# Eight experts in two stripes of 1792 columns: longer weight runs, eight slots of 14 KB, equal column groups

## What is computed

```python
def swiglu(h, w1, w3, w2):
    return (jax.nn.silu(h @ w1) * (h @ w3)) @ w2

def moe_ffn(h, router_w, w1, w3, w2):
    logits = (h @ router_w).astype(jnp.float32)
    vals, idx = lax.top_k(logits, TOP_K_EXPERTS)
    probs = jax.nn.softmax(vals, axis=-1)
    gate = jnp.sum(jax.nn.one_hot(idx, N_EXPERTS, dtype=jnp.float32) * probs[..., None], axis=-2)
    out = jnp.zeros_like(h)
    for e in range(N_EXPERTS):
        out = out + gate[..., e:e + 1] * swiglu(h, w1[e], w3[e], w2[e])
    return out
```

## Time and profile before

| | |
|---|---|
| Time, median of 3 runs | 1609.66 us (1607.83 to 1609.97) |
| Profiled execution, its own time | 1608.24 us |
| Its span, first to last instruction | 1606.5 us |
| Granted TensorE clock, mean | 0.992 |
| PE busy | 1569.4 us (98%) |
| DVE / ACT / POOL busy | 854.8 / 390.4 / 407.1 us |
| Moved by DMA | 481.74 MB, 300 GB/s over the span |

### The profile page before, as it was taken

How to read it: one execution, slowest core, us unless ns; L and a number is a source line. 1 busy time by engine, 2 the same in 40 slices (tenths; PEclk the granted TensorE clock), 3 DMA queues, 4 the chain that set the end, 5 groups by cost and what they waited for, 6 DMA issues and landing times.

```text
span 1606.5 us, 46001 instructions
## 1 busy us (share of the span) xinstructions
PE 1569.4 (98%) x20716; PEld 1466.1 (91%) x20716; DVE 854.8 (53%) x1453; ACT 390.4 (24%) x496; POOL 407.1 (25%) x541
## 2 busy tenths in 40 slices
PE   8999999999998999999999999999999999999998
PEld 5887888999988878899999999999999999999997
DVE  5799766455568986823434433533444334335235
ACT  4345455544454554520000000000000000000000
POOL 8966901899524244130000000000000000000100
PEclk9998999999999999999999999999999999999999
DMA  8543457556554535479999999999999999999996
GB/s 306 170 146 128 134 184 240 187 177 215 179 172 129 172 132 184 144 290 412 396 410 413 393 413 394 398 412 379 411 412 383 409 413 380 412 411 381 413 400 264
DMA packets 148647, 481.74 MB, mean 300 GB/s; under 512 B 7936, under 2 KB 32640, under 8 KB 133872
## 3 DMA queue, kind: packets, MB, share of 16 engines
q1 hardware_dynamic: 143968, 463.34, 76.2%
q0 software_dynamic: 4064, 14.95, 2.7%
q10 hardware_dynamic: 432, 0.65, 0.1%
HBM read 472.49 MB, written 6.42 MB: 298 GB/s over the span
## 4 chain that ended last, share of the span: by engine, by line
PE 55%; DMA 7%; DVE 6%; SPq 1%; issue 1%; ACT 0%; DVEq 0%
PE ps L1398 27%; PE ps L1395 16%; DMA raw<-moe_w 5%; DVE hidT L2652 4%; PE ps L737 2%; PE ps L739 2%; PE ps L738 2%; DMA ring_h<-moe_w 1%; DMA ring_w<-moe_w 1%; SPq L675 1%; PE ps L783 1%; PE ps L785 1%; PE ps L784 1%; DVE w_lo L331 1%; PE ps L973 1%
## 5 line engine op out<-in xcount | busy, mean ns | idle before, releaser
L2652 DVE STREAM_TRANSPOSE hidT<-hid_pair 32x128 f32<-32x128 f32 x660 | 276.9, 419 | 224.6 <-PE ps L1398 215.9
L331 DVE TENSOR_TENSOR w_lo<-raw,w_hi 128x2048 fp32r<-128x2048 f32 (+1 forms) x97 | 233.8, 2418 | 113.7 <-ACT w_hi L325 112.9
L1398 PE MATMUL ps<-ring_w,xgT 128*32 128x128 f32 x2352 | 261.1, 273 | 0.0
L1395 PE MATMUL ps<-ring_w,xgT 128*32 128x384 f32 x2352 | 257.8, 486 | 0.0
L1398 PEld LDWEIGHTS ps<-ring_w,xgT 128*32 128x32 f32 x2352 | 255.9, 110 | 0.0
L325 ACT ACTIVATE w_hi<-raw 128x2048 fp32r<-128x2048 f32 (+1 forms) x97 | 185.2, 1910 | 169.3 <-PE ps L739 82.8
L1398 PE MATMUL ps<-raw,xgT 128*32 128x128 f32 x1920 | 214.3, 273 | 0.0
L1395 PE MATMUL ps<-raw,xgT 128*32 128x384 f32 x1920 | 211.7, 486 | 2.4 <-DMA raw<-moe_w 2.3
L1398 PEld LDWEIGHTS ps<-raw,xgT 128*32 128x32 f32 x1920 | 208.8, 110 | 0.0
L2009 ACT ACTIVATE sil_pair<-ps 128x768 f32<-128x768 f32 (+1 forms) x32 | 23.4, 732 | 700.2 <-PE ps L1398 700.2
L2663 DVE TENSOR_TENSOR hid_pair<-sil_pair,ps 128x768 f32<-128x768 f32 (+1 forms) x32 | 27.3, 854 | 302.5 <-PE ps L1398 301.8
(11 more groups left out here) (429 smaller groups left out, 3174.7 us busy)
## 6 DMA issues: line engine op xcount, KB each, us to landing
raw<-moe_w SPq DMA_DIRECT2D x144, 1024.0 KB, 19.9
ring_w<-moe_w SPq DMA_DIRECT2D x144, 1024.0 KB, 20.6
ring_h<-moe_w SPq DMA_DIRECT2D x48, 1024.0 KB, 20.0
raw<-w_in SPq DMA_DIRECT2D x44, 1024.0 KB, 5.5
raw<-ffn_w SPq DMA_DIRECT2D x33, 1024.0 KB, 5.3
raw<-w_o SPq DMA_DIRECT2D x8, 1024.0 KB, 4.8
raw<-w_out_a SPq DMA_DIRECT2D x4, 1024.0 KB, 4.9
raw<-w_out_c SPq DMA_DIRECT2D x4, 1024.0 KB, 4.9
```

The lines of the kernel that those rows point to most:

```text
L331: dve.tensor_tensor(w_lo[:, n % SPLIT, 0:width], raw[:, n % RAW, 0:width], w_hi[:, n % SPLIT, 0:width].bitcast(F32), ALU.subtract)\
L1395: pe.matmul(ps[tile_rows(g), bank, 0:wide], x_of(g), w[:, 0:wide], start=first, stop=last, skip_group_check=True, tile_position=(0, TILE * g))
L1398: mm = pe.matmul(ps[SLOTS:P, bank, g * rest:(g + 1) * rest], x_of(g), w[:, wide:HALF], start=first and g == 0, stop=last, skip_group_check ...
L2652: ins = dve.transpose(turned[tile_rows(q), 4 * h:4 * h + 4, tile_rows(g)], src)
```

## The change

The experts go in two stripes (`MOE_STRIPES`) of 1792 columns (`MOE_W`). For a row of weights (one k of 128 input channels) the 1792 columns are four parts of 448 (`PART`). Part 0, 1 and 2 each have a bank: in bank `part` the groups 0 to 2 stream that part for the three tiles of tokens, and group 3 streams the last 448 columns for the tile of tokens with the number `part`. So every matmul of an up stage has 448 columns, 12 of them per row. Gate has banks 0 to 2, value 3 to 5, down 6 and 7; the gather and the token search, which had 6 and 7, share banks with gate, value or down, with new waits. Down weights are laid out so that a partition holds 14 consecutive rows of a stripe: `hid_pair` is read with a stride of 14 by the transposes (12 of 32x448 per stripe). The slots are 14 KB per partition (1.75 MiB), eight of them, in one buffer `ring` over the same memory as before. An up load is two k-rows of a stripe with runs of 7 KB, a down load 3.5 hidden rows with runs of 14 KB: 24 loads per expert. `raw_at` turns the earlier stages' slots so that the memory of the first ring slots comes free first; the first three loads wait for `lo_done` where the first six waited for `used`. The down matmuls (388 and 124 columns) are as they were, in another order of banks. In the diff below, removed lines that the kernel above shows are cut at some places, and so are parts that only rename.

```diff
+MOE_STRIPES = 2
+MOE_W = FF_EXPERT // MOE_STRIPES
+PART = MOE_W // 4
+HID = TILES * PART
+MOE_K = MOE_W // P
+MOE_CHUNK = 2 * MOE_W
+UPS = D // P // 2
+Y_BANK = 2 * TILES
+DOWNS = MOE_W * D // P // MOE_CHUNK
 MIX_CHUNKS = 35
 DENSE_CHUNKS = 3 * DENSE_STRIPES
-MOE_CHUNKS = 6 * sum(HALVES)
-RING = 14
+MOE_CHUNKS = MOE_STRIPES * (2 * UPS + DOWNS)
+RING = 8
...
+        with ExitStack() as experts_weights:
+            ring = sb("ring", [P, RING, MOE_CHUNK], F32, experts_weights)
...
-            w2e = moe_w2[0].rearrange("e (k p j) n -> p (e k) j n", p=P, j=4)
-            K2 = FF_EXPERT // HALF
+            w2e = moe_w2[0].rearrange("e (t p j) n -> p (e t) (j n)", p=P, j=MOE_K)
...
                 def load_ring(m, turns, src):
...
+                    r = m - MOE0
+                    if r < RING and isinstance(turns, int):
+                        end = -(-(r + 1) * MOE_CHUNK // CHUNK)
+                        if end > RAW + 2 * SPLIT:
+                            sp.wait_ge(S["gather_ps"], 2)
+                        if end > RAW:
+                            sp.wait_ge(used, MOE0)
+                        else:
+                            sp.wait_ge(lo_done, MOE0 - RAW + end)
                     else:
                         sp.wait_ge(used, value(sp, m - RING + 1 + RING * turns))
                     sp.dma_start(ring_view(m, tuple(src.shape[1:])), src).then_inc(ring_sem(m), 16)
                 def up(m, turns, w, e, t):
-                    ks = 4 // HALVES[t]
-                    for c in range(KD // ks):
-                        row = value(sp, KD * e + ks * c)
-                        load_ring(m + c, turns, w[:, bass.ds(row, ks), t * PAIR:t * PAIR + HALVES[t] * HALF])
+                    for c in range(UPS):
+                        row = value(sp, KD * e + 2 * c)
+                        load_ring(m + c, turns, w[:, bass.ds(row, 2), t * MOE_W:(t + 1) * MOE_W])
                 def down(m, turns, e, t):
-                    for c in range(2 * HALVES[t]):
-                        row = value(sp, K2 * e + 2 * t + c // 2)
-                        j = 2 * (c % 2)
-                        load_ring(m + c, turns, w2e[:, bass.ds(row, 1), j:j + 2, :].rearrange("p o j n -> p (o j) n"))
+                    for c in range(DOWNS):
+                        row = value(sp, MOE_STRIPES * e + t)
+                        load_ring(m + c, turns, w2e[:, bass.ds(row, 1), c * MOE_CHUNK:(c + 1) * MOE_CHUNK])
...
+                def up_row(bank, k, w):
+
+                    first, last = k == 0, k == KD - 1
+                    for part in range(TILES):
+                        for g in range(TILES):
+                            pe.matmul(ps[tile_rows(g), bank + part, 0:PART], xgT[:, k, tile_rows(g)],
+                                      w[:, part * PART:(part + 1) * PART], start=first, stop=last,
+                                      skip_group_check=True, tile_position=(0, TILE * g))
+                        mm = pe.matmul(ps[SLOTS:P, bank + part, 0:PART], xgT[:, k, tile_rows(part)],
+                                       w[:, TILES * PART:4 * PART], start=first, stop=last, skip_group_check=True,
                                        tile_position=(0, SLOTS))
                     return mm
...
                 def last_down(n, i, turns):
                     pe.wait_ge(S["hidT_made"], i - DENSE_STRIPES)
                     for half in range(2):
-                        for chunk in range(2):
-                            m = n + chunk
+                        for chunk in range(DOWNS):
                             if half == 0:
...
+                                loaded(n + chunk, turns)
+                            for q in halves_in(chunk):
+                                if q % 2 == half:
+                                    mm = down_half(half, last_hidT, q // 2, half_at(n, q), False,
+                                                   q // 2 == MOE_K - 1)
                             if half == 1:
                                 mm.then_inc(used, 1)
                         if half == 0:
                             mm.then_inc(S["y_half"], 1)
...
+                    n = n0 + 2 * UPS
                     pick_turned = last or rnd > 0
-                    step(n, i, turns, 2)
+                    if rnd > 0:
+                        pe.wait_ge(S["acc_done"], acc_before(rnd, e))
+                    up(n, 0, i + 1, turns, range(UPS // 2))
+                    pe.wait_ge(S["hid_done"], i + 1)
+                    if pick_turned:
+                        turn_pick(e)
+                    else:
+                        find_tokens(e + 1)
+                    up(n, 0, i + 1, turns, range(UPS // 2, UPS))
+                    if pick_turned:
+                        pe.wait_ge(S["pickT_done"], scattered_before(rnd, e) + 1)
+                    else:
+                        pe.wait_ge(S["token_done"], e + 1)
+                    up(n + UPS, 1, i + 1, turns)
+                    n += 2 * UPS
                     if rnd == 0:
                         pe.wait_ge(S["y_taken"], 1 + 4 * e)
...
+                    down(n, i + 1, turns, first=True)
+                    n += DOWNS
                     if last:
-                        last_down(n, i + 4, turns)
+                        last_down(n, i + 2, turns)
+                        pe.wait_ge(S["hid_done"], i + 2)
                     else:
                         if rnd == 0:
                             pe.wait_ge(S["xg_turned"], e + 1)
                         else:
+                            pe.wait_ge(S["sil_done"], i + 2)
+                            gather(e + 1, 0)
                             pe.wait_ge(S["xg_first"], gathers_before(rnd, e + 1) + 1)
                             pe.wait_ge(S["xg_second"], gathers_before(rnd, e + 1) + 1)
-                        step(n, i + 3, turns, 2)
-                        down(n + 8, i + 4, turns, 1)
+                        up(n, 0, i + 2, turns)
+                        up(n + UPS, 1, i + 2, turns)
+                        n += 2 * UPS
+                        down(n, i + 2, turns)
+                        if rnd > 0:
+                            pe.wait_ge(S["hid_done"], i + 3)
                     if pick_turned:
...
-                def turn_hidden(at, halves, free, dst=hidT):
+                def turn_hidden(at, free, dst=hidT):
                     dve.wait_ge(S["hid_done"], value(dve, at))
                     if free is not None:
                         dve.wait_ge(used, value(dve, free))
...
+                    turned = dst[:, :].rearrange("p (c s) -> p c s", s=SLOTS)
+                    for g in range(TILES):
+                        for q in range(4):
+                            rows = tile_rows(g if q < TILES else TILES)
+                            col = PART * (q if q < TILES else g)
+                            src = hid_pair[rows, col:col + PART].rearrange("s (n j) -> s j n", j=MOE_K)
+                            ins = dve.transpose(turned[tile_rows(q), :, tile_rows(g)], src)
                     ins.then_inc(S["hidT_made"], 1)
...
+                    n = n0 + 2 * UPS + MOE_CHUNKS * e
+                    if rnd == 0 and not last:
                         pick_slots(value(dve, e + 1), rnd)
-                    stripe(i + 2, n + 12, n + 20, 2, 2)
+                    turn_hidden(i + 1, n)
+                    if rnd > 0 and not last:
+                        dve.wait_ge(S["pickT_ps"], value(dve, scattered_before(rnd, e) + 1))
+                        pick_slots(value(dve, e + 1), rnd)
                     if rnd == 0 and not last:
                         tokens(e + 1)
-                    if last and rnd == 0:
-                        add_rows(0, 0)
-                    stripe(i + 3, n + 24, n + 28, 2, 1)
+                    if rnd == 0 and last:
+                        for k in range(2):
+                            for b in range(BLOCKS):
+                                add_rows(k, b)
+                    times_parts(i + 2, n + 2 * UPS, i + 1 - DENSE_STRIPES)
                     if last:
-                        turn_hidden(i + 4, 1, None, last_hidT)
-                        if rnd == 0:
-                            add_rows(0, 1)
-                            add_rows(1, 0)
+                        turn_hidden(i + 2, None, last_hidT)
                         y(e, 0)
-                        if rnd == 0:
-                            add_rows(1, 1)
                         y(e, 1)
                         add_to_x(e, True)
                         return
                     if rnd == 0:
-                        turn_gathered(e + 1, n + 28)
+                        turn_gathered(e + 1, n + 2 * UPS)
                     else:
-                        xg(e + 1)
-                    stripe(i + 4, n + 32, n + 40, 1, 2)
+                        xg(e + 1, 0)
+                    turn_hidden(i + 2, n + 2 * UPS + DOWNS)
+                    times_parts(i + 3, n + 4 * UPS + DOWNS, i + 2 - DENSE_STRIPES)
```

(25 more changed lines are left out.)

246 lines of the change are left out of this document (88 added, 158 removed).

## The result

The changed kernel takes 1596.15 us (median of 6 executions, 1594.67 to 1601.39), the kernel before 1609.62 beside it: ratio 0.992, 95% interval 0.9906 to 0.9935. The profiled execution takes 1595.35 us, its span is 1593.5.

The account below looks back on a forecast made before the run. TensorE was taken to bound the kernel, then slower weight loads after five and a half experts. 708.24 + 8 x 109.3 + a tail of 8.5 gave a span of 1591.1, as a time 1594 us; range 1590 to 1606.

Parts of the forecast that it names:

- The starvation: Experts, after five and a half of them: TensorE waits for weight loads, 10.0 us lost, to be regained.
- The pace: TensorE's time per expert when never starved: 109.3 us for 109.97, 5.3 us less over eight experts.
- the two losses named: TensorE's wait for hidT behind the short stripe (0.5 us per expert) and group 3's lag of 5 ns a pass; both go.
- D: Time the weight loads need per expert: 109.1 us with 7 and 14 KB runs, for 112.5; bounds 105.7 to 111.7.
- the prediction's own limit of 109.6: Load time per expert up to which the last landing is in time; each further us costs 7.6.
- the prediction's 7.6 experts: Experts' worth of loads behind the filled ring, used to forecast the last weight landing at 1567.2 for 1593.
- The fixed part of a run: Weight loads: each run costs a DMA engine a fixed 11 ns beside 0.0366 ns a byte.
- rival (a): Loads still end the kernel, at 109.6 to 111.4 us per expert: 1597 to 1606 us, chance 0.22.
- The rest at nothing: Transposes, silu, multiply, add_rows, first loads and tail: they stay hidden, no added time; transposes likely 12.6 us a stripe.
- The sum: Whole kernel: span 1591.1 us for 1606.5, 15.3 less in the profiled execution, time 1594.
- The ring: Weight slots: same memory as before, 36.6 us of TensorE's work, lead at the start some 12 us instead of 14.
- A near thing: End of the loads: last landing at 1567.2, wanted by 1571.2, 4 us to spare.

Follow-up runs that it names:

- after_short: Changed kernel with gate and value weights loaded in runs of 3.5 KB for 7 KB, same bytes and loads; 1607.67 us, 0.9988 of the kernel before.
- after_addrows: Changed kernel with the last expert's four add_rows moved from ahead of the last multiply to behind the last transposes; 1595.5 us, 0.9905 of the kernel before.
- after_down7: Changed kernel with down weights loaded in runs of 7 KB for 14 KB, same bytes and loads; 1594.98 us, 0.9894 of the kernel before.
- before_8k: Kernel before with gate and value weights loaded in 8 KB runs for 4 and 2 KB, same 42 loads; 1601.16 us, 0.9938 of the kernel before.
- after_14k: Changed kernel with gate and value weights loaded in runs of 14 KB for 7 KB, same bytes and loads; 1599.04 us, 0.9931 of the kernel before.
- ring4: Changed kernel with four 14 KB slots for eight, nothing else; 1601.05 us, 0.994 of the kernel before.

## Why the prediction was right

**The starvation: right.** 10.0 us in the sum, 9.8 by the kernel before with 8 KB runs, and 10.9 come back when the changed kernel gets short runs. Longer runs cure it in one kernel and shorter ones bring it back in the other.

**The pace: right, a little small.** 109.3 forecast, 109.21 measured: 8 x 0.74 = 5.9 us for 5.3. A pass of 448 columns takes what the line of 0.833 ns a column + 2.5 ns a piece says (375 ns), and the two losses named were the ones: 0.46 and 0.35 per expert, 0.66 together. The prediction knew 0.5 of the wait and gave the rest to the lag without a price of its own.

**D: the shift of the last landing right, in part by luck.** 109.1 forecast, 109.64 measured, beyond the prediction's own limit of 109.6. But the kernel before, by its landings, had 112.81 and not 112.5, which was read from one pair of searches that was only partly starved. What decides is the difference: 3.2 for 3.4. By the prediction's 7.6 experts that is a shift of 24.1 us; it was 885.4 - 857.7 = 27.7, as the first and the last expert gave more than the others. So two errors and the ends of the stream made up for one another, and the last landing came at 1566.6 for 1567.2. Against the last matmul of a kernel without waits (873.8) it had 16.1 us where `last_down` needs 11.4: 4.7 to spare, for 4 forecast.

The fixed part of a run, 11 ns in the prediction, is 9.1 between the changed kernel and its short runs (2.33 us for 256 runs per engine), 9.1 from there to 14 KB (1.16 for 128), 7.8 between the kernels with 8 KB and with 4 KB (2.24 for 288), and only 2.5 where the down weights went from 14 to 7 KB (0.16 for 64). So it is not one constant, but for up weights 8 to 9. Run length is not all of D either: the kernel with 8 KB runs has 336 runs for the changed kernel's 320, worth 0.15 us, and a D that is 0.93 higher. Fewer instruction fetches (11 per expert for 16) may hold a part of that; no run separates it. The rule of the Trainium skill that the prediction weighed (*DMA: Bandwidth & Descriptors*, section *Why small descriptors are slow*), 3 cycles or 3.5 ns a packet, would put after_short 0.9 over the changed kernel, by estimate; it is 2.3 over it. The rows were the better guide, and rival (a) did not come.

**The rest at nothing: wrong in one term.** Transposes take 948 ns, 11.4 us a stripe, for 1050 and 12.6, `silu` 1.29 and the multiply 1.55 as forecast. The failed step is "expert 6's rows leave at 1503.6, the last gather is issued 14 us later and lands in 12.8, so they end 32 us into a stretch of 36". The 12.8 was a median of four, whose last took 16.5, and it was measured beside runs of at most 8 KB; beside 14 KB runs the last took 24.0. `add_rows` came after the last value matmul, and the last matmul 875.7 - 873.8 = 1.9 us late. after_addrows and after_down7 remove it by two ways and give the same 873.8.

**The sum.** In spans 15.4 less were forecast, 13.0 were found. 10.0 + 5.9 - 1.9 = 14.0, and the last matmul moved by 889.8 - 875.7 = 14.1, counted from the first gate matmul. The first gate matmul came 0.64 later and the tail was 8.9 for 8.5: 14.1 - 0.6 - 0.4 = 13.1. In times, 1596.15 for 1594.

**The ring.** "A near thing", in the prediction, rested on the end of the stream, and there were 4.7 us to spare; the lead inside the stream was never short, as six slots show. The slots do move the last landing: it came 2.9 us later with six and 11.5 later with four. A load is issued when TensorE frees its slot, so each slot less issues it 4.55 us later (9.1 and 18.2), and the shorter time from issue to landing in the last expert (11.6 and 11.5 us for 18.1) gives 6.5 and 6.6 back: 2.6 and 11.6. The prediction took the last landing from D alone.

## What to carry to other kernels

Where DMA bounds or nearly bounds a kernel, compare the landing of the same load from one period to the next, for that shows whether the lead shrinks before anybody is starved. Look at the time from issue to landing beside it: where that stays the same, the loads keep the compute engine's pace (six slots here), and D says nothing of what they could do. When the runs of the main stream get longer, look at the small transfers beside it: they take turns with it by packets, and each turn has become longer. Put work that waits for such a transfer behind the work that feeds the bound engine, not ahead of it.

## What the runs showed of the hardware

**With a deep queue half of a load lands late.** In the kernels with eight slots and up runs of 7 KB or less, and in those with the 14 slots of before, the last weights arrive at half rate, with a DMA share of 0.5: for 7 us in the changed kernel, 12 in before_8k. With six slots there is no such stretch, and none with four or in after_14k. Changed kernel, before_8k, six slots (us, busy PE, clock, DMA share, GB/s):

```profile
1558.00:1565.00 7.00, 6.47 (x117) 1.00 0.50 209
```

```profile
1564.00:1576.00 12.00, 11.87 (x221) 1.00 0.50 207
```

```profile
1562.00:1568.00 6.00, 5.60 (x104) 1.00 1.01 425
1568.00:1570.00 2.00, 2.00 (x42) 1.00 0.67 280
```

The landing marks tell more. Of the sixteen marks of the changed kernel's last load eight come from 1557.5 to 1558.6 and eight from 1565.2 to 1566.6. The gap between the two halves is 0.1 us in the first expert and 6.6 in the last; with six slots it stays at 0.5 or less. From one expert to the next the first half of the marks is 108.6 apart and the second 109.64: D is the pace of the slower half. Even halves would have brought the last landing some 3 us sooner, an estimate from half of the 6.6. Which engines are slower, why, and why the slower half keeps 109.2 when six slots hold the faster half back, no run shows.

**A short starvation can cost the clock.** Stretches of 1 us at the end of after_short (busy PE, clock, DMA share, GB/s):

```profile
1574.00:1575.00 1.00, 1.00 (x24) 1.00 1.05 432
...
1579.00:1580.00 1.00, 1.00 (x23) 1.00 0.51 215
1580.00:1581.00 1.00, 0.14 (x4) 1.00 0.50 215
1581.00:1582.00 1.00, 0.00 (x0) 1.00 0.47 201
...
1584.00:1585.00 1.00, 1.00 (x16) 0.50 0.40 172
1585.00:1586.00 1.00, 1.00 (x16) 0.50 0.17 72
...
1587.00:1588.00 1.00, 1.00 (x24) 1.00 0.00 0
```

TensorE stood still for 2.1 us (1580.1 to 1582.2), and then the granted clock was 0.50, 1.2 GHz, for some 3 us, with 16 matmuls a us for 24. ring4 shows the same behind a wait of 2.2 us, three us at 0.50. At half the clock 3 us hold 1.5 us of work, which is part of what ring4 lost beyond its 4.0 us of waits; some 1.2 of its 6.7 stay open. But the length of the wait does not decide it: the wait of 3.9 us in after_short (1533.7 to 1537.6) and that of 3.2 in after_14k (1565.4 to 1568.6) were followed by a granted clock of 1.00, like the 1.7 of the changed kernel. Behind the first of them:

```profile
1537.00:1542.00 5.00, 4.42 (x48) 1.00 1.04 410
```

What else decides, no run shows.
